# Up-units of the second feed-forward layer multiplied in products of 256 columns

## The chip, the cores and the metric

The kernel runs on one core of one Trainium2 chip. The metric is the device time of one execution in microseconds, from the start of the program to its end. Lower is better.

## What is computed

A two-layer transformer stem (a dilated-attention layer and a latent-attention layer, each followed by a feed-forward network) and then one block of another model, on 512 tokens of width 1024 in float32. The change touches the second of the two feed-forward networks alone:

```
D_MODEL = 1024
SEQ = 512
D_FF = 4 * D_MODEL

def sq_relu_mlp(h, w1, w2):
    a = jax.nn.relu(h @ w1)
    return (a * a) @ w2

        h = rms_norm(x, norm_ffn[i])
        x = x + sq_relu_mlp(h, ffn_w1[i], ffn_w2[i])
```

`h @ w1` is 512 x 1024 by 1024 x 4096; the change is in how half of the tiles of this product are issued for layer `i = 1`.

## The kernel before

**Data.** Everything is kept transposed: a tile has 128 features on the partitions and the 512 tokens along the columns. All weights come as a stream of units of 128 x 1024 (512 KB); each unit is loaded by SyncE into one of four slots of `raw`, rounded to the short format fp32r by ScalarE (`w_hi`, L1069), and what the rounding left is made by VectorE (`w_lo`, L1734). Activations are kept in the same two parts: `h_hi`/`h_lo` for the first feed-forward layer, `g_hi`/`g_lo` for the second.

**A product.** A weight tile of 128 x 128 times a tile of activations is three matmuls of 512 columns into one PSUM bank, in `mm3`: high weights by high activations (L432), high weights by low activations (L433), low weights by high activations (L434). The program has no weight load of its own: each of these calls becomes a weight load (LDWEIGHTS, the engine PEld of the profile) and a matmul (MATMUL, the engine PE). The high weights are loaded for L432 and again for L433. `pairs` reads the columns of the activations in an order that puts column `b` beside column `256 + b`. In other stages the operands are plain float32; a call with such operands shows as two loads and two matmuls.

**A unit.** `unit` waits until the unit's `w_lo` is there and then does the eight tiles of the unit: 24 matmuls of 512 columns, of which the last one tells ScalarE that the bank is ready.

**The feed-forward layer.** `ffn(layer, i)` is one of four chunks: eight up-units (`j` 0 to 7, hidden columns of `h @ w1`) and eight down-units (`j` 8 to 15, of `(a*a) @ w2`). Units 0 and 1 are done together, tile by tile, by `units_together`, as are units 8 and 9; the others go through `unit`. After an up-unit ScalarE takes the bank through the relu (`f_r`, L1199), VectorE squares it (`f_s`, L1921), ScalarE rounds it (`f_hi`, L1204) and VectorE makes the rest (`f_lo`, L1924); units 8 and 9 read these eight tiles in turn. Chunks 1 and 2 of the four are two rounds of a loop, chunks 0 and 3 are written out. Between the up-units 1 and 2 of chunk 0 stand four float32 matmuls that sum squares (L468, L473).

What sets the order is only the order of the program on each engine and the semaphores between them. Nothing is planned or rearranged.

Of the kernel before, what the change touches and what calls it, by code (L numbers as in the profile page):

```python
# [27 lines left out]
KT = D // P  # L28
# [47 lines left out]
def slot(u):  # L76
    if u < R2:
        return u % 3
    return (u - R2) % 4
# [31 lines left out]
def build(nc, stream, x_in, cols_in, crow_in, lam_in, pos_in, ada_in, gate_in, rope_in, consts_in, mask_in, out, stop="all"):  # L111
    with ExitStack() as ctx:
# [6 lines left out]
        def fixed(name, shape, dt=F32):  # L119
            t = at(name, shape, base[0], dt)  # L120
            n = 4
            for s in shape[1:]:
                n *= s
            base[0] += (n + 31) // 32 * 32
            return t
# [11 lines left out]
        w_hi = fixed("w_hi", [P, 4, UNIT], F32R)  # L137
        w_lo = fixed("w_lo", [P, 4, UNIT], F32R)
# [96 lines left out]
        def bank(b, n=512, o=0):  # L235
            return psum[:, b, o:o + n]


        S = {}
# [27 lines left out]
        def after(name, idx):  # L267

            v = idx + 1 + CREDIT.get(name, 0)
            return S[name], (max(v, 0) if isinstance(v, int) else v)  # L270
# [14 lines left out]
        def tile_of(t, sl, w):  # L285
            return t[:, sl, w * P:(w + 1) * P]
# [3 lines left out]
        def pairs(t):  # L290
            return t.rearrange("p (a b) -> p b a", a=2)
# [43 lines left out]
        FFN_IN = ((h_hi, h_lo), (g_hi, g_lo))  # L335
# [90 lines left out]
        def _(pe):  # L426
            credits(pe, "mm", "A_T", "A_PV")

            def mm3(o, whi, wlo, xh, xl, start, stop, read=pairs):

                xh, xl = read(xh), read(xl)
                nc.tensor.matmul(o, whi, xh, start=start, stop=False)  # L432
                nc.tensor.matmul(o, whi, xl, start=False, stop=False)  # L433
                return nc.tensor.matmul(o, wlo, xh, start=False, stop=stop)  # L434

            def unit(u, sl, o, xh, xl, ready=None):

                pe.wait_ge(*after("lo", u))
                for k in range(KT):
                    if ready:  # L440
                        pe.wait_ge(*ready(k))
                    last = mm3(o, tile_of(w_hi, sl, k), tile_of(w_lo, sl, k), xh[:, k, :], xl[:, k, :], k == 0, k == KT - 1)
                last.then_inc(S["mm"], 1)

            def units_together(u, slots, outs, xh, xl, ready, turn=range(KT)):

                pe.wait_ge(*after("lo", u + len(slots) - 1))
                for k in turn:
                    pe.wait_ge(*ready(k))
                    for sl, o in zip(slots, outs):  # L450
                        last = mm3(o, tile_of(w_hi, sl, k), tile_of(w_lo, sl, k), xh[:, k, :], xl[:, k, :], k == turn[0], k == turn[-1])
                        if k == turn[-1]:
                            last.then_inc(S["mm"], 1)
# [7 lines left out]
            def collected_sums(kind, nn):  # L461
                collected_first(kind, nn)
                collected_last(kind, nn)
# [18 lines left out]
            def idle_before(nn):  # L482

                idle(5)
                idle(4, after("N_rst", nn))
                idle(3, after("N_hi", 8 * nn))

            def norm_ready(nn):
                return lambda k: after("N_lo", 8 * nn + k)
# [71 lines left out]
            def a_head(h, par, project=True, attend=True):  # L561
                for j in range(9):
                    n = 9 * h + j
                    if project:
                        pe.wait_ge(*after("A_evac", n - 2))
                        unit(U_A + n, j % 3, bank((par + j) % 2), h_hi, h_lo)
                        if j >= 1:
                            a_post(h, j - 1, par)
                    if attend:
                        if j == 0:  # L570
                            a_post(h - 1, 8, 1 - par)
                        if j in (0, 2):
                            a_scores(h - 1, j, 1 - par)
                        if j in (2, 4):
                            a_transposes(h - 1, j - 2)
                            a_transposes(h - 1, j - 1)
                        if j in (4, 6):
                            a_values(h - 1, j - 4)
                            a_values(h - 1, j - 3)


            def outward(u0, xh, xl, ready, free, kind, nn, b0=0, begun=False, turn=range(KT), first=2):

                if not begun:
                    pe.wait_ge(*free(1))
                    if first > 2:
                        pe.wait_ge(*free(2))
                    units_together(u0, [slot(u0 + i) for i in range(first)], [bank((b0 + i) % 4) for i in range(first)],
                                   xh, xl, ready, turn)
                for o in range(first, KT):  # L590
                    pe.wait_ge(*free(o))
                    unit(u0 + o, slot(u0 + o), bank((o + b0) % 4), xh, xl)
                if kind == "Y":
                    collected_sums(kind, nn)


            def ffn(layer, i, first=False, last=False):
                u0 = (U_F0, U_F1)[layer]
                c = 4 * layer + i
                for j in range(16):  # L600
                    if first and j in (0, 2):
                        pe.wait_ge(*after("R_x", 8 * layer + 5 + j))

                    if j < 4:
                        pe.wait_ge(*after("F_x", 8 * c + j - 4))
                    elif j < 12:
                        pe.wait_ge(*after("F_s", 8 * c + j - 4))
                    else:
                        pe.wait_ge(*after("F_x", 8 * c + j - 12))
                    sl = slot(u0 + j)  # L610
                    if j == 1:
                        units_together(u0 + 16 * i, (slot(u0), sl), (bank(0), bank(1)), *FFN_IN[layer], norm_ready(1 + 2 * layer))
                        if first:
                            collected_sums("N", 1 + 2 * layer)
                    elif 2 <= j < 8:
                        unit(u0 + 16 * i + j, sl, bank(j % 4), *FFN_IN[layer])
                    elif j == 9:
                        units_together(u0 + 16 * i + 8, (slot(u0 + 8), sl), (bank(0), bank(1)), f_hi, f_lo,
                                  lambda k: after("F_lo", 8 * c + k))
                    elif j >= 10:  # L620
                        unit(u0 + 16 * i + j, sl, bank(j % 4), f_hi, f_lo)
                if last and layer == 1:
                    collected_sums("N", 4)
                    idle_before(4)
# [118 lines left out]
            a_out(1, 7)  # L743
            outward(U_AO, a_oh, a_ol, None, lambda o: after("R_x", o - 4), "N", 1, begun=True)
            ffn(0, 0, first=True)
            with pe.Fori(1, FFN_CHUNKS - 1) as i:
                ffn(0, i)
            ffn(0, FFN_CHUNKS - 1, last=True)


# [252 lines left out]
            for n in range(2, 20):  # L1003
                u = U_MI + n
                pe.wait_ge(*after("M_ev", n - 2))
                pe.wait_ge(*after("lo", u))
                for k in range(KT):
# [9 lines left out]
                    if at_step in SOFT_AT:  # L1017
# [5 lines left out]
                        if m >= 2:  # L1023
                            c_values(m - 2)
                    last = mm3(bank(n % 2), tile_of(w_hi, slot(u), k), tile_of(w_lo, slot(u), k), h_hi[:, k, :], h_lo[:, k, :],
                               k == 0, k == KT - 1)
# [1580 lines left out]
```

## Time and profile before

| what | value |
|---|---|
| time, median of 3 runs | 2382.67 us (2382.32 to 2382.8) |
| span of the profiled execution, first to last instruction | 2380.2 us |
| TensorE matmul (PE) busy | 2336.3 us, 98% of the span |
| weight loads (PEld) busy | 1981.6 us, 83% |
| VectorE busy | 1440.3 us, 61% |
| ScalarE busy | 1038.3 us, 44% |
| matmuls and weight loads | 11342 of each |

The profiled execution's own time is given as its span; the time of a run also holds what lies outside the first and last instruction, 2.5 us between this span and the median. A matmul's bar in the trace is longer than its share of the time, because the next one begins while it still drains: the step from one start to the next is what counts, not the bar. The times of weight loads overlap with those of matmuls.

### The profile page before, as it was taken

The page shows a single profiled execution, that of the slowest core. Times are in us where ns is not written, and L with a number is a line of the kernel's source. Part 1 is how long each engine was busy: PE and PEld are TensorE (multiplying, and loading weights), DVE is VectorE, ACT ScalarE, POOL GpSimd, SP SyncE. Part 2 cuts the span into 40 slices and gives each one's busy share as a digit, 9 for nine tenths or more (in the row PEclk, how much of TensorE's full clock was granted, in tenths as well). Part 3 has the DMA queues.
Part 4 walks back from the last instruction along what each step waited for, and adds up shares of the span by engine and source line. Part 5 has one row for each costly group of instructions (what it writes and reads, how often), then busy time and mean ns, then how long its engine had stood idle before and what let it go on. Part 6 is the DMA issues. An engine that isn't in the chain of part 4 may idle for free.

```text
span 2380.2 us, 30886 instructions
## 1 busy us (share of the span) xinstructions
PE 2336.3 (98%) x11342; PEld 1981.6 (83%) x11342; DVE 1440.3 (61%) x2073; ACT 1038.3 (44%) x1562; POOL 0.2 (0%) x4
## 2 busy tenths in 40 slices
PE   7999999999999999999999999999999999999999
PEld 5788888888888886888888888888877677888887
DVE  7877777767566677867566575333356986433333
ACT  5655555544233347854223333323346565322333
POOL 0000000000000000000000000000000000000000
PEclk9999999999999999999999999999999999999999
DMA  4222222235444531024444533332322112323231
GB/s 156 80 80 80 79 79 77 77 103 177 140 161 159 174 117 64 1 72 168 159 150 159 177 102 108 105 100 95 115 71 67 58 54 71 97 94 110 93 111 54
DMA packets 71246, 249.57 MB, mean 105 GB/s; under 512 B 9824, under 2 KB 10336, under 8 KB 70752
## 3 DMA queue, kind: packets, MB, share of 16 engines
q1 hardware_dynamic: 68912, 247.28, 31.1%
q8 instruction: 74, 1.21, 0.2%
q10 hardware_dynamic: 2224, 0.79, 0.1%
q14 instruction: 36, 0.29, 0.0%
HBM read 245.94 MB, written 2.10 MB: 104 GB/s over the span
## 4 chain that ended last, share of the span: by engine, by line
PE 91%; DVE 5%; ACT 3%; issue 1%; DMA 0%; SPq 0%; ACTq 0%; DVEq 0%
PE psum L432 27%; PE psum L434 27%; PE psum L433 27%; PE psum L496 2%; PE psum L885 1%; PE psum L527 1%; PE psum L556 1%; PE psum L549 1%; PE psum L939 1%; DVE w_lo L1734 1%; PE psum L989 1%; DVE x L2249 0%; PE psum L969 0%; PE psum L532 0%; DVE y L2247 0%
## 5 line engine op out<-in xcount | busy, mean ns | idle before, releaser
L432 PE MATMUL psum<-h_hi,w_hi 128*128 128x512 f32 x1768 | 681.6, 386 | 7.6 <-DVE w_lo L1734 2.7
L433 PE MATMUL psum<-h_lo,w_hi 128*128 128x512 f32 x1768 | 670.1, 379 | 0.0
L434 PE MATMUL psum<-h_hi,w_lo 128*128 128x512 f32 x1768 | 670.1, 379 | 0.0
L1069 ACT ACTIVATE w_hi<-raw 128x1024 fp32r<-128x1024 f32 x385 | 403.2, 1052 | 454.8 <-PE psum L434 445.0
L1734 DVE TENSOR_TENSOR w_lo<-raw,w_hi 128x1024 fp32r<-128x1024 f32 x385 | 466.0, 1220 | 133.3 <-ACT w_hi L1069 131.9
L432 PEld LDWEIGHTS psum<-h_hi,w_hi 128*128 128x128 f32 x1768 | 334.2, 189 | 62.5 <-issue 9.3
L433 PEld LDWEIGHTS psum<-h_lo,w_hi 128*128 128x128 f32 x1768 | 334.3, 189 | 47.6 <-issue 2.6
L434 PEld LDWEIGHTS psum<-h_hi,w_lo 128*128 128x128 f32 x1768 | 334.2, 189 | 47.4
L2227 DVE TENSOR_TENSOR s_s<-s_g,psum 128x512 f32<-128x512 f32 x44 | 30.3, 688 | 275.6 <-issue 224.2
L432 PE MATMUL psum<-f_hi,w_hi 128*128 128x512 f32 x512 | 194.0, 379 | 0.0
L433 PE MATMUL psum<-f_lo,w_hi 128*128 128x512 f32 x512 | 194.0, 379 | 0.0
L434 PE MATMUL psum<-f_hi,w_lo 128*128 128x512 f32 x512 | 194.0, 379 | 0.0
L432 PE MATMUL psum<-s_hi,w_hi 128*128 128x512 f32 x352 | 133.4, 379 | 0.0
L433 PE MATMUL psum<-s_lo,w_hi 128*128 128x512 f32 x352 | 133.4, 379 | 0.0
L434 PE MATMUL psum<-s_hi,w_lo 128*128 128x512 f32 x352 | 133.4, 379 | 0.0
L1199 ACT ACTIVATE f_r<-psum 128x512 f32<-128x512 f32 x64 | 38.1, 595 | 207.6 <-PE psum L434 207.5
L1948 DVE TENSOR_TENSOR nrm<-psum,rst 128x512 f32<-128x512 f32 x64 | 44.2, 691 | 128.2 <-PE psum L434 128.0
L434 PEld LDWEIGHTS psum<-f_hi,w_lo 128*128 128x128 f32 x512 | 96.8, 189 | 13.8
L432 PEld LDWEIGHTS psum<-f_hi,w_hi 128*128 128x128 f32 x512 | 96.8, 189 | 13.7
L433 PEld LDWEIGHTS psum<-f_lo,w_hi 128*128 128x128 f32 x512 | 96.8, 189 | 13.7
L1921 DVE TENSOR_TENSOR f_s<-f_r,psum 128x512 f32<-128x512 f32 x64 | 43.9, 686 | 101.5 <-ACT f_r L1199 101.4
L1224 ACT ACTIVATE s_g<-psum 128x512 f32<-128x512 f32 x44 | 26.2, 596 | 175.6 <-PE psum L434 175.6
(343 smaller groups left out, 3252.8 us busy)
## 6 DMA issues: line engine op xcount, KB each, us to landing
raw<-stream SPq DMA_DIRECT2D x385, 512.0 KB, 3.5
ada_raw<-ada_in SPq DMA_DIRECT2D x72, 512.0 KB, 4.0
x<-x_in SPq DMA_DIRECT2D x2, 1024.0 KB, 6.4
out<-x SPq DMA_DIRECT2D x8, 256.0 KB, 2.4
a_mask<-mask_in SPq DMA_DIRECT2D x1, 1024.0 KB, 9.4
crow<-crow_in SPq DMA_DIRECT2D x2, 512.0 KB, 4.5
gatew<-gate_in ACTq DMA_DIRECT2D x2, 256.0 KB, 3.7
a_cos<-rope_in SPq DMA_DIRECT2D x1, 256.0 KB, 7.8
```

The source lines that it names most:

```text
L432: nc.tensor.matmul(o, whi, xh, start=start, stop=False)
L433: nc.tensor.matmul(o, whi, xl, start=False, stop=False)
L434: return nc.tensor.matmul(o, wlo, xh, start=False, stop=stop)
L496: last = nc.tensor.transpose(o[:, b * P:(b + 1) * P], src[:, b * P:(b + 1) * P], ident[:])
L527: nc.tensor.matmul(psum[32 * t:32 * t + 32, 2 + r % 2, 0:256], q[:, 0, r * P + 32 * t:r * P + 32 * t + 32], a_k0[:, par, t * P:t * P + 256 ...
L1069: A(w_hi[:, slot(u0), :], raw[:, slot(u0), :], ACT.Copy).then_inc(S["hi"], 1)
L1199: A(stored(f_r[:, j % 2, :]), by_parity(bank(j % 4)), ACT.Relu).then_inc(S["F_r"], 1)
L1224: A(stored(s_g[:, q % 2, :]), by_parity(bank(j % 6)), ACT.Silu).then_inc(S["Sw_g"], 1)
L1734: V.tensor_tensor(w_lo[:, sl, :], raw[:, sl, :], f32(w_hi[:, sl, :]), ALU.subtract).then_inc(S["lo"], 1)
L1921: V.tensor_tensor(stored(f_s[:, j % 2, :]), stored(f_r[:, j % 2, :]), by_parity(bank(j % 4)), ALU.mult).then_inc(S["F_s"], 1)
L1948: V.tensor_tensor(nrm[:, 1, :], down, rst[:, 1, :], ALU.mult).then_inc(S["F_t"], 1)
L2227: V.tensor_tensor(stored(s_s[:, q % 2, :]), stored(s_g[:, q % 2, :]), by_parity(bank((2 * jj + 1) % 6)), ALU.mult).then_inc(S["Sw_s"], 1)
```

## The change

For the second layer alone (`layer == 1`) the up-units with `j` from 2 to 7 go through a new function, `unit_halves`. It issues the same three products for each weight tile, but each of them as two matmuls of 256 columns, the first half of the bank and then the second half, one behind the other with the same weights. Units 0 and 1, the down-units and the first layer are as before. No wait, no semaphore and no buffer changes.

```diff
+            def mm3_halves(o, whi, wlo, xh, xl, start, stop):
+
+                xh, xl = pairs(xh), pairs(xl)
+                for w, x_, first, last in ((whi, xh, start, False), (whi, xl, False, False), (wlo, xh, False, stop)):
+                    for c in range(2):
+                        b = slice(c * 128, (c + 1) * 128)
+                        ins = nc.tensor.matmul(o[:, c * 256:(c + 1) * 256], w, x_[:, b, :], start=first and c == 0, stop=last and c == 1,
+                                               skip_group_check=True)
+                return ins
+
+            def unit_halves(u, sl, o, xh, xl):
+
+                pe.wait_ge(*after("lo", u))
+                for k in range(KT):
+                    last = mm3_halves(o, tile_of(w_hi, sl, k), tile_of(w_lo, sl, k), xh[:, k, :], xl[:, k, :], k == 0, k == KT - 1)
+                last.then_inc(S["mm"], 1)
+
...
                     elif 2 <= j < 8:
-                        unit(u0 + 16 * i + j, sl, bank(j % 4), *FFN_IN[layer])
+                        (unit, unit_halves)[layer](u0 + 16 * i + j, sl, bank(j % 4), *FFN_IN[layer])
```

The order on TensorE where chunk 0 of the second layer passes from the sums of squares to up-unit 2, before (a row is a line of the program, what is written and read, and the shape; weight loads are not listed):

```order
L468 MATMUL psum<-nrm,ones 128x512
L473 MATMUL psum<-sq,ones 128x512
L432 MATMUL psum<-g_hi,w_hi 128x512
L433 MATMUL psum<-g_lo,w_hi 128x512
L434 MATMUL psum<-g_hi,w_lo 128x512
```

The same place of the changed program, in which the sums have the lines L485 and L490 and x2 is two matmuls in a row:

```order
L485 MATMUL psum<-nrm,ones 128x512
L490 MATMUL psum<-sq,ones 128x512
L442 MATMUL psum<-g_hi,w_hi 128x256 x2
L442 MATMUL psum<-g_lo,w_hi 128x256 x2
L442 MATMUL psum<-g_hi,w_lo 128x256 x2
```

Each matmul of 512 columns has become two of 256 in its own place; nothing else stands between them.

The order on TensorE where up-unit 7 of a chunk ends and down-units 8 and 9 begin, before:

```order
L432 MATMUL psum<-g_hi,w_hi 128x512
L433 MATMUL psum<-g_lo,w_hi 128x512
L434 MATMUL psum<-g_hi,w_lo 128x512
L432 MATMUL psum<-f_hi,w_hi 128x512
L433 MATMUL psum<-f_lo,w_hi 128x512
```

And in the changed program:

```order
L442 MATMUL psum<-g_hi,w_hi 128x256 x2
L442 MATMUL psum<-g_lo,w_hi 128x256 x2
L442 MATMUL psum<-g_hi,w_lo 128x256 x2
L432 MATMUL psum<-f_hi,w_hi 128x512
L433 MATMUL psum<-f_lo,w_hi 128x512
```

The down-units follow as before, in matmuls of 512 columns. Per chunk 6 units of 24 products are affected, in four chunks 576 products: 1152 matmuls and 1152 weight loads stand in the place of 576 of each. The instructions of the other engines are the same.

## Rows read from the trace of the kernel before

**Rows 1.** The page: busy time per engine, and the granted clock in 40 slices.

```profile
PE 2336.3 (98%) x11342; PEld 1981.6 (83%) x11342; DVE 1440.3 (61%) x2073; ACT 1038.3 (44%) x1562; POOL 0.2 (0%) x4
...
PEclk9999999999999999999999999999999999999999
```

**Rows 2.** The page: the chain that ended last, by engine.

```profile
PE 91%; DVE 5%; ACT 3%; issue 1%; DMA 0%; SPq 0%; ACTq 0%; DVEq 0%
```

**Rows 3.** Windows: busy us and count per engine, clock; layer two, then two dense stretches.

```profile
1078.00:1413.00 335.00, 334.82 (x1546) 291.74 (x1544) 211.93 (x279) 106.12 (x140) 0.00 (x0) 1.00 0.46 156
497.50:503.87 6.37, 6.37 (x65) 4.76 (x65) 3.72 (x12) 1.79 (x5) 0.00 (x0) 1.00 0.03 9
496.54:508.91 12.37, 12.15 (x101) 9.67 (x100) 6.38 (x22) 5.80 (x13) 0.00 (x0) 1.00 0.09 34
```

**Rows 4.** Tile g_hi: duration min/median/max in ns, first and last start in us.

```profile
L432 PEld LDWEIGHTS psum<-g_hi,w_hi x256: 189/189/190, 1078.4 to 1369.5; 128*128 128x128 f32 x128
L432 PE MATMUL psum<-g_hi,w_hi x256: 379/379/780, 1078.6 to 1369.7; 128*128 128x512 f32 x128
```

**Rows 5.** Timeline of weight loads in an up-unit: start us, duration us.

```profile
1109.85 0.19 PEld L432 LDWEIGHTS psum<-g_hi,w_hi 128*128 128x128 f32 x1
1110.07 0.19 PEld L433 LDWEIGHTS psum<-g_lo,w_hi 128*128 128x128 f32 x1
```

**Rows 6.** Timeline of matmuls at the same place.

```profile
1109.63 0.38 PE L433 MATMUL psum<-g_lo,w_hi 128*128 128x512 f32 x1
1109.85 0.38 PE L434 MATMUL psum<-g_hi,w_lo 128*128 128x512 f32 x1
...
1112.87 0.38 PE L433 MATMUL psum<-g_lo,w_hi 128*128 128x512 f32 x1
```

**Rows 7.** The chain in order of time: start us, us, what; short and long float32 matmuls.

```profile
98.38 0.87 PE psum L496 x8
...
364.48 1.79 PE psum L556 x16
...
958.58 0.89 PE psum L885 x8
...
1089.09 0.86 PE psum L468 x2
1089.95 0.86 PE psum L473 x2
...
1800.15 3.43 PE psum L939 x8
```

**Rows 8.** Timeline of weight loads from plain float32 (L885) to fp32r (L862, L863).

```profile
958.31 0.97 PEld L885 LDWEIGHTS psum<-b_pt,b_v 128*128 128x128 f32 x8
959.20 0.19 PEld L862 LDWEIGHTS psum<-b_kh,h_hi 128*128 128x128 f32 x1
959.31 0.19 PEld L863 LDWEIGHTS psum<-b_kl,h_hi 128*128 128x128 f32 x1
959.53 0.19 PEld L864 LDWEIGHTS psum<-b_kh,h_lo 128*128 128x128 f32 x1
```

**Rows 9.** Timeline of weight loads after a wait of TensorE.

```profile
34.50 0.19 PEld L432 LDWEIGHTS psum<-h_hi,w_hi 128*128 128x128 f32 x1 [0.27 <-DVE h_lo L1765]
34.61 0.19 PEld L433 LDWEIGHTS psum<-h_lo,w_hi 128*128 128x128 f32 x1
```

**Rows 10.** Timeline of ScalarE and VectorE behind up-unit 7 of chunk 0.

```profile
1121.92 0.60 ACT L1199 ACTIVATE f_r<-psum 128x512 f32<-128x512 f32 x1 [3.12 <-PE psum L434]
...
1126.04 0.68 DVE L1924 TENSOR_TENSOR f_lo<-f_s,f_hi 128x512 fp32r<-128x512 f32 x1
```

**Rows 11.** Waits from 1078 to 1413 us: total us, times, longest; then SyncE's own.

```profile
ACT f_r L1199 <- PE psum L434: 104.0, 27, 12.9
ACT w_hi L1069 <- PE psum L434: 86.5, 18, 9.2
DVE nrm L1948 <- PE psum L434: 67.0, 27, 3.8
...
SPq L368 <- DVE w_lo L1734: 185.5, 63, 7.5
```

**Rows 12.** DMA queues from 1078 to 1161 us: packets, MB, share of 16 engines.

```profile
q8 instruction: 3, 0.05, 0.3%
```

## The prediction

> **What bounds the kernel now.** I read the page first. TensorE is busy for 98% of the span, the chain that ended last lies on it for 91%, and its granted clock stands at the full level, 2.4 GHz, in every slice [rows 1, 2]. The windows view of the stage that changes says it more sharply: from 1078 to 1413 us TensorE is busy for 334.82 of 335.00 us [rows 3]. The waits there are all of others for TensorE: ScalarE's relu waits 104.0 us for matmuls, VectorE 67.0 us, and SyncE holds its loads back for free slots for 185.5 us [rows 11]. So whatever the changed matmuls gain or lose is gained or lost in full, and only the step from one matmul to the next matters.
>
> That step is read from starts, not from bars. Fifteen steps of 512 columns take 1112.87 - 1109.63 = 3.24 us, 216 ns each [rows 6]. A long baseline gives it closer. From the first to the last L432 on `g_hi`, 1078.6 to 1369.7 us [rows 4], lie three chunks of 384 products and 64 tiles less one of three more, 1341 products, and the two pairs of sums of 0.86 us each [rows 7]: (291.1 - 1.72) / 1341 = **215.8 ns**. A load starts when the matmul before its own starts (both rows at 1109.85 us) [rows 5, 6], so a load has 215.8 ns to be ready in, and is never what is waited for.
>
> **The change part by part.** It takes away 576 matmuls of 512 columns with their loads, and puts 1152 of 256 columns with 1152 loads in their place. Nothing else moves. Call h the step of a half; the change costs 576 x (2h - 215.8 ns). The trace has no full-array matmul of 256 columns, so h is put together from what a step must contain, and is the longer of two things.
>
> *The stream of columns.* For plain float32 the trace has the same engine at two widths: eight transposes of 128 columns in 0.87 us, 108.8 ns each, and eight passes of 512 columns in 3.43 us, 428.8 ns each [rows 7]. That is 0.833 ns for a column and some 2 ns per matmul. The fp32r matmul takes half as long per column: 215.8 ns are 512 x 0.4167 = 213.3 ns and 2.5 ns. So 256 columns stream in 106.7 + 2.5 = 109.2 ns. A half can't go below 106.7 ns even if the 2.5 ns vanished; that would be 576 x (213.3 - 215.8) = -1.4 us, 0.06%, so a gain that can be told from nothing is excluded by the column rate.
>
> *The load of the weights.* Each half loads its 128 x 128 tile again, as L433 does now right behind L432 with the same `w_hi` tile [rows 5]. How long must a load be awaited? After an idle TensorE, L432's load starts at 34.50 us and the next one, which marks the start of L432's stream, at 34.61 [rows 9]: 110 ns. In the bursts of short float32 matmuls, whose own stream would allow 109 ns, the step is longer: 0.89 us for eight (L885) and 1.79 us for sixteen (L556) [rows 7]. Rounding allows 110.6 to 111.9 ns by the first row and 111.6 to 112.2 ns by the second; both hold between 111.6 and 111.9, and I take 111.7 ns. The transposes with the same columns and a step of 108.8 ns show that the stream isn't what makes 111.7; the load is. An fp32r load costs the same: L862's load starts at 959.20 us and its stream at 959.31 [rows 8].
>
> A half of 256 columns is therefore in the same position as a float32 pass of 128: stream 109.2 ns, load 111.7 ns, and the load decides by a little. h = 111.7 ns: 2 x 111.7 - 215.8 = 7.6 ns per product, x 576 = **4.4 us**. With the last half of a unit the next load is of a 512-column matmul and costs the same 111.7 ns, so nothing is to be added at the seams.
>
> The Trainium skill, "TensorE: Matmul & The Clock Gate", section "Back-to-back issue gap", gives N / 2.4 + 2.5 ns at full clock, from which the stream alone would follow: 109.2 ns for a half, and 1.5 us for the change. The trace agrees with it at 512 columns (215.8 ns) and disagrees at L885, whose step is 111.7 ns for reasons outside that formula. The same section names sustained steps for pairs of load and matmul, 81 ns at 128 columns and 131 ns at 512, which would speak against halving; the 215.8 ns of this trace contradict the second of them.
>
> *What comes at no cost.* The last up-unit ends at 1121.92 us, and its `f_lo` is done at 1126.04 + 0.68 = 1126.72 us [rows 10]. Units 8 and 9 need it only for their eighth tile, after 42 products, 42 x 0.2158 = 9.1 us, at 1131.0 us: 4.3 us of cover, which the change leaves alone, as the down-units keep their pace. If it were gone, each microsecond missing would cost one per chunk, 4 in all. Up-units become slower by 24 x 7.6 ns = 0.18 us each, so ScalarE, VectorE and the loads have that much more time and none is later for TensorE. Instruction fetches: three packets in a chunk take 0.3% of 16 engines' 83 us, some 4 us, 1.3 us each [rows 12]. With the instructions twice as dense one is needed about every 14 us in place of 28 us, and 1.3 us still fit ten times.
>
> **Sum.** The profiled span is 2380.2 us and the median 2382.67, 2.5 us outside the instructions that the change doesn't touch. 2380.2 + 4.4 + 2.5 = **2387.1 us**, 0.18% over now. What a measurement of this kernel can tell from no change is about 0.2%, 4.8 us. The forecast stands just inside it.
>
> **The rivals.**
>
> *The stream decides.* If a half is paced by its columns, or if the second load of the same tile overlaps more than those of L885, h is 109.2 ns and the cost 576 x 2.6 ns = 1.5 us: 2384.2 us. For it: the loads after an idle engine took 110 ns or a little less [rows 9], nearer to 109. Against it: every dense burst of loads that are not transposes reads 111.7 ns. Chance 0.11.
>
> *The instructions aren't supplied fast enough* (the slower side). A unit now asks for a load and a matmul each 111.7 ns for 5.4 us on end; now it is 215.8 ns. What the trace shows beyond short bursts: 65 matmuls and 65 loads in 6.37 us, 98 ns a pair, and 101 in 12.37 us, 122 ns a pair [rows 3]. The first speaks against this rival, but some of its instructions may have been waiting ready from the slower stretch ahead, and six units on end take 32 us. If the 122 ns of the longer stretch were the supply's, the change would cost 576 x (244.9 - 215.8) = 16.8 us: 2399.5 us. It decides, and passes 0.2%, from a supply step of 112.1 ns. The Trainium skill, in "What happens when you issue a matmul" of "TensorE: Matmul & The Clock Gate", names some 62 ns per matmul where its sequencer decodes in software; for a load and a matmul that would be 124 ns, about the same 2401 us, and the 98 ns of the first stretch are against it. Chance 0.12.
>
> *The load is slower behind a stream at full rate.* All bursts that show 111.7 ns have float32 streams, which take a column in 0.833 ns. Behind an fp32r stream, at twice that rate, a load is only known to be done within 215.8 ns. Were both to share what they read with, h would lie between 111.7 and 215.8 ns; at the upper end the cost is 576 x 215.8 = 124 us: 2507 us. Against it: the loads' bars are 189 ns behind fp32r streams, and no longer behind float32 ones (8 bars with 7 steps of 111.7 fill the 0.97 us of L885 with 0.19 for one) [rows 5, 8]. It too passes 0.2% from h = 112.1 ns. Chance 0.10.
>
> *Something downstream gets earlier or later* by more than I see, either way: 0.05, of it 0.02 for faster.
>
> **How the numbers follow.** The forecast, load-paced, has 0.62, with its own range of 2386.0 to 2388.2 us (h from 111.3 to 112.3 ns with the readings' rounding). The stream's 2384.2 and the milder half of the supply's and the load's cases, up to about 10 us over now, bring it to 8 in 10: 2384.0 to 2393.0 us. Slower by over 0.2%: both slower rivals 0.22, a fifth of the forecast's own 0.62 that ends above 2387.4, 0.12, and 0.02 from downstream, 0.36. Faster by over 0.2%: 0.02. The rest, 0.62, is within 0.2%.
>
> **What would show it.** In the profile after, L442 has 1152 matmuls and as many loads; in the timeline of loads inside an up-unit 2 to 7 of layer two, steps of 111 or 112 ns with no idle of PEld between them. Steps of 109 ns would be the stream; steps that are even at 109 to 112 for the first microseconds of a unit and then longer, with PE idle on issue, the supply; even steps well above 112, the slowed load. The stage from unit 2 to the last chunk's unit 7 grows by 4.4 us and nothing outside it. The forecast is wrong if h is off: each nanosecond of h is 1.15 us.

## The result and the profile after

The changed kernel takes 2386.41 us (median of 18 runs, 2385.55 to 2386.99), the kernel before 2382.22 us in the same comparison (18 runs, 2381.27 to 2382.8). The ratio is 1.0018, with a 95% interval of 1.0011 to 1.0025: 4.2 us slower, between 2.6 and 6.0. The forecast was 4.4 us.

The page of the changed kernel answers to [rows 1, 2]:

```profile
span 2385.0 us, 32038 instructions
...
PE 2341.1 (98%) x11918; PEld 2001.7 (84%) x11918; DVE 1440.1 (60%) x2073; ACT 1040.1 (44%) x1562; POOL 0.2 (0%) x4
...
PEclk9999999999999999999999999999999999999999
...
PE 91%; DVE 5%; ACT 3%; issue 1%; DMA 0%; SPq 0%; ACTq 0%; DVEq 0%
```

There are 576 more matmuls and 576 more loads (11918 against 11342), and TensorE is busy 4.8 us longer; VectorE's and ScalarE's busy times are within 2 us of what they were, and the clock is as it was. The windows view of the stage, as in [rows 3]:

```profile
1078.00:1417.40 339.40, 339.40 (x2124) 311.98 (x2122) 211.63 (x278) 106.47 (x140) 0.00 (x0) 1.00 0.47 155
```

TensorE still never stops in it. How long the stage is, is read from the tiles. The last matmul of the stage on `f_hi` in the kernel before:

```profile
L432 PE MATMUL psum<-f_hi,w_hi x512: 379/379/379, 592.4 to 1411.2; 128*128 128x512 f32 x171
```

Tile `f_hi` of the changed kernel, with duration min/median/max in ns and first and last start in us:

```profile
L432 PE MATMUL psum<-f_hi,w_hi x512: 379/379/382, 592.8 to 1416.0; 128*128 128x512 f32 x171
```

Tile `g_hi` of the same kernel:

```profile
L442 PEld LDWEIGHTS psum<-g_hi,w_hi x384: 189/192/192, 1090.7 to 1374.5; 128*128 128x128 f32 x192
L442 PE MATMUL psum<-g_hi,w_hi x384: 272/275/673, 1090.8 to 1374.6; 128*128 128x256 f32 x192
...
L432 PE MATMUL psum<-g_hi,w_hi x64: 379/379/379, 1079.1 to 1342.4; 128*128 128x512 f32 x64
```

From the first L432 on `g_hi` to the last on `f_hi` it was 1411.2 - 1078.6 = 332.6 us [rows 4] and is 1416.0 - 1079.1 = 336.9 us: 4.3 us more. The rest of the span's 4.8 us is half a microsecond ahead of the stage, which begins at 1079.1 us in place of 1078.6. Kernels that are the same up to there differ by more: below, the first half of a product starts at 1090.0 us in the run with uneven pieces and at 1091.0 in the one with thirds.

The timeline of weight loads in a middle up-unit, where [rows 5] had one load every 216 ns:

```profile
1109.36 0.30 PEld L442 LDWEIGHTS psum<-g_lo,w_hi 128*128 128x128 f32 x2
1109.59 0.30 PEld L442 LDWEIGHTS psum<-g_hi,w_lo 128*128 128x128 f32 x2
...
1111.37 0.30 PEld L442 LDWEIGHTS psum<-g_lo,w_hi 128*128 128x128 f32 x2
```

From 1109.36 to 1111.37 us lie 18 loads: 2.01 / 18 = 0.1117, **111.7 ns a step**, with no idle of PEld in between. The x2 are the two halves, and a row's 0.30 is one step of 0.11 and one bar of 0.19.

The waits of the stage:

```profile
ACT w_hi L1086 <- PE psum L434: 86.7, 18, 9.2
ACT f_r L1216 <- PE psum L442: 73.0, 23, 3.3
DVE nrm L1965 <- PE psum L434: 66.9, 27, 3.8
DVE f_s L1938 <- ACT f_r L1216: 56.6, 23, 7.9
ACT f_r L1216 <- PE psum L434: 35.0, 4, 12.9
```

The longest are for TensorE, as in [rows 11]; the fourth is VectorE's for ScalarE's relu. No wait of TensorE is among them. ScalarE's relu waits 73.0 + 35.0 = 108.0 us in place of 104.0, about what TensorE has become slower.

### The profile page after: what moved, and what is told of

It reads as the page before. It is cut to its first block, busy times and chain, and to the rows that moved or that the text cites. A ratio compares the mean times of both kernels' runs of the same rounds, so it can differ in the third digit from the quotient of the medians.

```text
span 2385.0 us, 32038 instructions
## 1 busy us (share of the span) xinstructions
PE 2341.1 (98%) x11918; PEld 2001.7 (84%) x11918; DVE 1440.1 (60%) x2073; ACT 1040.1 (44%) x1562; POOL 0.2 (0%) x4
## 4 chain that ended last, share of the span: by engine, by line
PE 91%; DVE 5%; ACT 3%; issue 1%; DMA 0%; SPq 0%; ACTq 0%; DVEq 0%
PE psum L432 25%; PE psum L433 25%; PE psum L434 25%; PE psum L442 5%; PE psum L513 2%; PE psum L902 1%; PE psum L544 1%; PE psum L573 1%; PE psum L566 1%; PE psum L956 1%; DVE w_lo L1751 1%; PE psum L1006 1%; DVE x L2266 0%; PE psum L986 0%; PE psum L549 0%
## 5 line engine op out<-in xcount | busy, mean ns | idle before, releaser
L432 PE MATMUL psum<-h_hi,w_hi 128*128 128x512 f32 x1768 | 682.3, 386 | 7.5 <-DVE w_lo L1751 2.7
L1086 ACT ACTIVATE w_hi<-raw 128x1024 fp32r<-128x1024 f32 x385 | 404.2, 1054 | 454.4 <-PE psum L434 445.1
L432 PEld LDWEIGHTS psum<-h_hi,w_hi 128*128 128x128 f32 x1768 | 334.6, 189 | 62.6 <-issue 9.3
L432 PE MATMUL psum<-f_hi,w_hi 128*128 128x512 f32 x512 | 194.1, 379 | 0.0
L432 PE MATMUL psum<-s_hi,w_hi 128*128 128x512 f32 x352 | 133.4, 379 | 0.0
L432 PEld LDWEIGHTS psum<-f_hi,w_hi 128*128 128x128 f32 x512 | 96.8, 189 | 13.6
L433 PEld LDWEIGHTS psum<-f_lo,w_hi 128*128 128x128 f32 x512 | 96.8, 189 | 13.6
```

Of the source, the lines that this page charges most:

```text
L1086: A(w_hi[:, slot(u0), :], raw[:, slot(u0), :], ACT.Copy).then_inc(S["hi"], 1)
```

## The experiments

The measured interval, 2.6 to 6.0 us, leaves out the 1.5 us of a half paced by its stream, but not a cost that each half has for another reason: the forecast rests on a difference of 2.5 ns, 109.2 ns for the stream and 111.7 ns for the load. Three theories were told apart. **Load-paced**: a step is the longer of the weight load (111.7 ns for 128 columns of weights) and the stream (0.4167 ns a column and 2.5 ns). **Fixed cost**: every matmul of a cut product costs 5.0 ns on top of its columns, whatever the load (a whole product shows 2.5 ns). **Supply**: a load and a matmul can't be had faster than every 111.7 ns. Each kernel below is the changed kernel with another edit; all but `all_halves` change the same 24 units alone.

Uneven pieces, thirds, quarters and the quarters with 64 and with 96 columns of weights were executed once each, and the kernel before scatters from 2381.0 to 2382.7 us. So the length of the stage, read in every profile from the first L432 on `g_hi` to the last on `f_hi`, stands beside the times:

| kernel | stage, us | more than before | by load-paced |
|---|---|---|---|
| before | 332.6 | | |
| the change | 336.9 | 4.3 | 4.3 |
| uneven pieces | 366.2 | 33.6 | 33.6 |
| thirds | 401.2 | 68.6 | 68.7 |
| quarters | 470.3 | 137.7 | 133.1 |
| quarters, loop written out | 465.6 | 133.0 | 133.1 |
| halves, 64 columns of weights | 334.0 | 1.4 | 1.5 |
| whole products, 64 columns | 332.6 | 0.0 | 0.0 |
| quarters, 64 columns | 347.7 | 15.1 | 10.0 |
| quarters, 96 columns, written out | 404.2 | 71.6 | 71.5 |
| half by half | 337.0 | 4.4 | 4.3 |

The last column takes 58.3 and 85.0 ns, the steps found below, for loads of 64 and 96 columns. Two rows stand out, by 4.6 and 5.1 us; both are taken up under "The loop".

**Uneven pieces.** The pieces have 384 and 128 columns; as many matmuls, loads and columns as in the change.

```diff
-                    for c in range(2):
-                        b = slice(c * 128, (c + 1) * 128)
-                        ins = nc.tensor.matmul(o[:, c * 256:(c + 1) * 256], w, x_[:, b, :], start=first and c == 0, stop=last and c == 1,
+                    for c, (p, q) in enumerate(zip([0, 192, 256], [0, 192, 256][1:])):
+                        ins = nc.tensor.matmul(o[:, 2 * p:2 * q], w, x_[:, p:q, :], start=first and c == 0, stop=last and c == 1,
...
```

> The pieces of a product are 384 and 128 columns instead of two of 256; the same count of matmuls and loads. Load-paced (step = the longer of a weight load, 111.7 ns, and columns x 0.4167 + 2.5 ns): 162.5 + 111.7 = 274.2 ns a product, 576 x (274.2 - 215.8) = 33.6 us, about 2415.8 us. Fixed cost per matmul (columns x 0.4167 + 5.0 ns, no limit by the load): 223.3 ns as with even halves, 2386.5 us. Supply of instructions at 111.7 ns a pair: as load-paced.

Measured: 2415.23 us against 2381.68 before, 33.6 us more. The weight loads of a middle up-unit:

```profile
1109.47 0.30 PEld L441 LDWEIGHTS psum<-g_lo,w_hi 128*128 128x128 f32 x2
...
1110.84 0.30 PEld L441 LDWEIGHTS psum<-g_hi,w_hi 128*128 128x128 f32 x2
```

Five products in 1.37 us, 274 ns each, which is the sum that load-paced gives: 162.5 ns for the long piece and 111.7 for the short one. The fixed cost falls. By this theory what is lost is the room behind the short piece: its columns need 56 ns, and the next load isn't there before 111.7. The rows shown give the sum alone, not how the two pieces share it.

**Thirds and quarters.** The same edit with the cuts `[0, 86, 171, 256]` and `[0, 64, 128, 192, 256]`.

> Three matmuls of 172, 170 and 170 columns in the place of each of 512. Load-paced: 3 x 111.7 = 335.1 ns, 576 x 119.3 = 68.7 us, 2450.9 us. Fixed cost: 228.3 ns, 7.2 us, 2389.4 us. If fp32r streams of less than 256 columns took the 0.833 ns per column of plain float32: 145.8 + 2 x 144.1 = 434 ns, 125.7 us, 2507.9 us.

> Four matmuls of 128 columns in the place of each of 512. Load-paced: 4 x 111.7 = 446.8 ns, 576 x 231.0 = 133.1 us, 2515.3 us. Fixed cost: 213.3 + 4 x 5.0 = 233.3 ns, 10.1 us, 2392.3 us. Supply: as load-paced.

Measured: thirds 2451.26 us, 69.4 us over the 2381.87 before; quarters 2520.09 us, 138.4 us over 2381.68. Weight loads of thirds:

```profile
1109.41 0.41 PEld L441 LDWEIGHTS psum<-g_hi,w_hi 128*128 128x128 f32 x3
...
1110.75 0.41 PEld L441 LDWEIGHTS psum<-g_lo,w_hi 128*128 128x128 f32 x3
```

And of quarters:

```profile
1109.37 0.53 PEld L441 LDWEIGHTS psum<-g_hi,w_lo 128*128 128x128 f32 x4
...
1110.71 0.41 PEld L441 LDWEIGHTS psum<-g_hi,w_lo 128*128 128x128 f32 x3
```

In both it is 12 steps in 1.34 us, 111.7 ns, for pieces of 170 or 172, of 128 and, in the change, of 256 columns. Down to 128 columns an fp32r stream doesn't become slow enough to matter. Quarters took 5.3 us more than 576 x (4 x 111.7 - 215.8) = 133.1 us; that is taken up below.

**Fewer columns of weights.** Load-paced and supply agree on all of this. A load of 64 columns parts them. In `halves_64_weights` the pieces are even halves, in `quarters_64_weights` quarters, in `whole_64_weights` whole products. These kernels leave out half of the output rows of the 24 units. The edit, against the form with cuts:

```diff
-                        ins = nc.tensor.matmul(o[:, 2 * p:2 * q], w, x_[:, p:q, :], start=first and c == 0, stop=last and c == 1,
+                        ins = nc.tensor.matmul(o[0:64, 2 * p:2 * q], w[:, 0:64], x_[:, p:q, :], start=first and c == 0, stop=last and c == 1,
```

> Even halves, but the weights of each are only columns 0 to 63 of the tile, so the output rows 64 to 127 of these units are left out; matmuls stream the same 256 columns. Load-paced: a load of half the columns takes some 58 ns and no longer decides, the step falls to the stream's 109.2 ns, a product to 218.4 ns, cost 1.5 us, 2383.7 us. Fixed cost or supply: the step stays at 111.7 ns, 2386.5 us.

> A control for the run with 64 columns of weights: whole products of 512 columns with weights of 64 columns (output rows 64 to 127 of these units left out). All theories: 215.8 ns a product, the time of before, 2382.2 us.

> Quarters of 128 columns with weights of 64 columns (output rows 64 to 127 of these units left out). Load-paced: load some 58 ns, stream 128 x 0.4167 + 2.5 = 55.8 ns, step 58 ns, product 233 ns, 10 us, 2392 us. Supply at 111.7 ns a pair: 133 us, 2515 us. Narrow fp32r streams at 0.833 ns per column: step 109.2 ns, 127 us, 2509 us.

Measured: halves 2383.27 us (ratio 1.0007, 0.9998 to 1.0016), whole 2382.03 us (1.0001, 0.9992 to 1.001), both against 2381.68; quarters 2396.92 us, 15.0 us over 2381.87. The intervals of the first two overlap, so it is their traces that decide: the stage of whole products is as long as before, 332.6 us, so fewer columns of weights alone change nothing, and that of halves is 334.0 us. Weight loads of halves with 64 columns of weights:

```profile
1109.44 0.24 PEld L441 LDWEIGHTS psum<-g_lo,w_hi 128*64 128x64 f32 x2
...
1110.75 0.24 PEld L441 LDWEIGHTS psum<-g_lo,w_hi 128*64 128x64 f32 x2
```

And of quarters with 64 columns of weights:

```profile
1109.58 0.31 PEld L441 LDWEIGHTS psum<-g_lo,w_hi 128*64 128x64 f32 x4
...
1110.98 0.14 PEld L441 LDWEIGHTS psum<-g_lo,w_hi 128*64 128x64 f32 x1
```

The halves' step is 1.31 / 12 = 109.2 ns: with the load out of the way it is the stream's, and 576 x (2 x 109.2 - 215.8) = 1.5 us is what the stage has grown by. The quarters' is 1.40 / 24 = 58.3 ns, just above the 55.8 ns of 128 columns. So a load and a matmul can be had every 58 ns, and the supply isn't what makes 111.7. The time is 15.0 us over, where 576 x (4 x 58.3 - 215.8) = 10.0 us was expected; the rest is the loop's, as in quarters.

**A third point for the load.** Quarters with weights of 96 columns, and the loop written out (see below).

> As quarters_written_out, with weights of 96 columns (output rows 96 to 127 of these units left out). If the load takes its columns / 1.2 + 5 ns, as 111.66 ns at 128 and 58.33 ns at 64 say, the step is 85.0 ns, a product 340 ns, 576 x 124.2 = 71.5 us, about 2453 us.

Measured: 2453.75 us, 72.1 us over 2381.7. Its weight loads:

```profile
1109.55 0.42 PEld L441 LDWEIGHTS psum<-g_lo,w_hi 128*96 128x96 f32 x4
...
1110.91 0.25 PEld L441 LDWEIGHTS psum<-g_hi,w_lo 128*96 128x96 f32 x2
```

1.36 / 16 = 85.0 ns. With 58.3, 85.0 and 111.7 ns for 64, 96 and 128 columns of weights the load is on a line: 0.833 ns a column and 5.0 ns.

This line holds for the loads of ordinary matmuls. The transposes have loads of 128 columns too, and a step of 108.8 ns that is shorter than 111.7. Their loads differ: in the kernel before, the mean bar of a load (the second number between the strokes, in ns) is 141 for a transpose and 192 for a dense burst of float32 matmuls.

```profile
L556 PEld LDWEIGHTS psum<-a_pt,a_v 128*128 128x128 f32 x128 | 14.9, 192 | 0.0
L496 PEld LDWEIGHTS psum<-ident,a_s 128*128 128x128 f32 x128 | 14.7, 141 | 1.3 <-DVE a_s L1841 0.5
```

Why a transpose's load is shorter was not tried.

**The order of the halves.** First the three matmuls of the first half, then those of the second.

```diff
-                for w, x_, first, last in ((whi, xh, start, False), (whi, xl, False, False), (wlo, xh, False, stop)):
-                    for c in range(2):
-                        b = slice(c * 128, (c + 1) * 128)
+                for c in range(2):
+                    b = slice(c * 128, (c + 1) * 128)
+                    for w, x_, first, last in ((whi, xh, start, False), (whi, xl, False, False), (wlo, xh, False, stop)):
...
```

> The three matmuls of the first half of the columns, then the three of the second half: the same tile is loaded twice in a row less often (2 of 6 loads repeat the load before, in place of 4 of 6). Load-paced with every load done in full: the same as the change, 2386.4 us. If a repeated load were cheaper or dearer than a new one, the time moves by 576 x the difference / 3 or so.

Measured: 2386.1 us against 2381.87, ratio 1.0018 (1.0008 to 1.0027), as the change, and the stage is as long to a tenth or so of a microsecond. This order makes 384 of the 1152 halves load a new tile where the change repeats one (the expectation's third of 576 is too low). A half can't go below its stream's 109.2 ns, so a cheaper repeat could have shown as 384 x 2.5 ns = 1.0 us at most, at the edge of what the times tell. Quarters show it better: three of their four loads repeat the one before behind a stream of 56 ns, and each takes 111.7 ns. A load that repeats the one before is as dear as a new one.

**Everything in halves.** `mm3` hands all its paired products to `mm3_halves`, in all stages.

```diff
             def mm3(o, whi, wlo, xh, xl, start, stop, read=pairs):
 
+                if read is pairs:
+                    return mm3_halves(o, whi, wlo, xh, xl, start, stop)
```

> All products of mm3 that read in pairs are done in halves, in both layers and everywhere else: 9120 matmuls of 512 columns become 18240. Load-paced: 9120 x 7.5 ns = 68 us, 2450.6 us, a little less where TensorE now waits for others. Supply that falls behind in long dense stretches: clearly more than that, with PE idle on issue.

Measured: 2458.55 us against 2381.87, ratio 1.0321 (1.0301 to 1.0342), 76.7 us more. The profile has 20534 - 11342 = 9192 more matmuls, so 9192 products were halved, where the expectation had 9120; load-paced gives 68.9 us, and 7.8 us are left. The waits of TensorE name a place:

```profile
PE psum L444 <- issue: 7.4, 4, 2.8
```

Four times, 7.4 us in all, it had nothing to do and waited for nothing that the profile shows; before, there was no such row for its matmuls. One of them in the timeline:

```profile
329.32 0.60 PE L515 MATMUL psum<-ident,a_raw 128*128 128x128 f32 x4
332.74 0.79 PE L444 MATMUL psum<-h_hi,w_hi 128*128 128x256 f32 x2 [2.82 <-issue]
```

**The loop.** Quarters have one such stop of 2.6 us, where chunk 2, the second round of the loop over chunks 1 and 2, has just begun. So have quarters with 64 columns of weights, at 1255.74 us, of 2.71 us. The timeline of quarters:

```profile
1314.49 0.38 PE L432 MATMUL psum<-g_hi,w_hi 128*128 128x512 f32 x1
1317.51 0.48 PE L433 MATMUL psum<-g_lo,w_hi 128*128 128x512 f32 x1 [2.63 <-issue]
...
1318.44 0.63 PE L433 MATMUL psum<-g_lo,w_hi 128*128 128x512 f32 x1
1318.87 0.63 PE L434 MATMUL psum<-g_hi,w_lo 128*128 128x512 f32 x1
...
1321.67 0.38 PE L432 MATMUL psum<-g_hi,w_hi 128*128 128x512 f32 x1
```

And the windows of quarters there:

```profile
1314.70:1317.30 2.60, 0.17 (x1) 0.00 (x0) 1.19 (x2) 0.00 (x0) 0.00 (x0) 1.00 0.30 72
1317.30:1321.00 3.70, 3.49 (x9) 2.79 (x10) 0.00 (x0) 0.00 (x0) 0.00 (x0) 0.60 0.37 132
```

After the stop the granted clock falls to 1.2 GHz (0.60 in the mean of the second window), and a step of 512 columns is 1318.87 - 1318.44 = 0.43 us, twice as long. The stop puts 3.02 us in the place of one step of 0.22, and the 11 steps behind it take 4.16 us in place of 2.37: 2.8 and 1.8 us, 4.6 of the 4.7 by which the stage is longer than with the loop written out.

The DMA view names what else is particular to that round. Its queue q8 carries instructions, in packets of 16 KB. In the second round of quarters, 1312 to 1420 us:

```profile
q8 instruction: 8, 0.13, 0.5%
```

And within the stop alone, 1314.7 to 1317.4 us:

```profile
q8 instruction: 1, 0.02, 2.2%
```

In the second round of the kernel before (1244 to 1327 us), of the change (1245 to 1328), of thirds (1282 to 1390) and of the feed-forward loop of `all_halves` (1280.7 to 1378) the view has no packet of q8 at all. So the instructions of those rounds are not loaded a second time, and those of quarters are. That TensorE's stop is the wait for the first of these packets fits both views, but no row names it as what ended the wait.

One kernel more takes the loop away from the second layer and leaves all else of quarters:

```diff
             ffn(1, 0, first=True)
-            with pe.Fori(1, FFN_CHUNKS - 1) as i:
+            for i in range(1, FFN_CHUNKS - 1):
                 ffn(1, i)
```

> As quarters, with the four chunks of the second layer written out on TensorE in place of the loop over chunks 1 and 2. Steps stay at 111.7 ns. If the 5 us that quarters took beyond 4 x 111.66 ns a product are the fetch of instructions at the start of the loop's second round (2.6 us of idle, then matmuls at 1.2 GHz), they are gone: about 2515 us. If they come from dense instructions as such, 2520 us as before.

Measured: 2514.82 us against 2381.7, 133.1 us more, to the tenth what 4 x 111.7 ns give, and no wait on issue in its profile. The surplus was the loop's. Written out, the instructions come in packets all along (13 from 1195 to 1430 us) without a stop, so loading as such doesn't stop TensorE; it does where it falls on the start of a round. The round of quarters has 96 + 1152 + 384 = 1632 loads and matmuls; the rounds of thirds (1344), of the feed-forward chunks in `all_halves` (1536), and of the change (1056) show no such stop. The four stops of `all_halves` are in the loop over the heads: two at the start of its second round (202.32 and 205.67 us) and two at that of its third (332.74 and 335.81 us). Its round grew from about 1350 loads and matmuls, for which the kernel before loads no packet of q8 in the last two rounds, to about 2210. These two rounds take 260.2 us (199.06 to 459.25) in place of 240.1 (196.82 to 436.94), of which their 864 halved products are 6.5; the stops and the lower clock behind them (0.50 from 202.9 to 209.7 us) make the other 13.6. The rest of the kernel grew by some 6 us less than load-paced gives; the expectation had foreseen less where TensorE waits for others, but how much of it that is was not traced.

## Why the prediction was right

**The bound.** TensorE alone sets the time of the stage: right; 339.40 us busy of 339.40, and 576 products at 7.5 ns more come out in the end in full. The sentence that the waits there are all for TensorE was too wide: the same view of the kernel before also has VectorE waiting 52.4 us for ScalarE's relu and ScalarE 24.7 us for VectorE. None of them is a wait of TensorE, so the sum doesn't depend on it.

**The step of a half.** 111.7 ns, taken from bursts of float32 matmuls [rows 7]: right to the tenth, 2.01 us for 18 loads. That it is the load which makes it, and not the stream or a cost per matmul, was argued from the transposes' 108.8 ns. The argument holds only because the loads of transposes are shorter, which the prediction didn't say: a load of 111.7 ns would have paced them too. It is now shown: with 64 columns of weights the step falls to 109.2 ns, the value given for the stream. The float32 passes of 128 columns were the right stand-in, since they have the same load and a stream as long.

**The sum.** 576 x 7.6 ns = 4.4 us; the stage grew by 4.3 us, the medians lie 4.2 us apart. The absolute 2387.1 us is 0.7 above the measured 2386.41; 0.45 us of that is that the kernel before came out at 2382.22 in this comparison and not 2382.67. The forecast's own range was given too wide: h from 111.3 to 112.3 ns makes 3.9 to 5.1 us, 2386.6 to 2387.8 us.

**What was said to cost nothing** did. The relu behind up-unit 7 of chunk 0 starts at 1123.52 us and its `f_lo` is done at 1128.33, 4.8 us later, as it was before [rows 10]; down-unit 8 begins at 1123.32 us and needs it after 9.1 us, so 4.1 us of cover are left. The prediction's 4.3 us were counted from the relu's start, 0.2 us behind that of the down-unit. It also spread the loading of instructions evenly over the chunks. That cost the forecast nothing, but it isn't so: the second round of the loop loads none here, and loads them anew, with a stop, once the round is long enough.

**The rivals.** *The stream decides*: fell, by the steps. *The supply*: fell for the instructions in a row, since 58.3 ns a pair hold through whole units, against the 122 and 124 ns by which it was priced. It exists in a form that the prediction didn't have: at the start of a loop's later rounds, when the round is long enough; the change's isn't. The 122 ns of [rows 3] were the mix of that stretch, not a limit. *The slower load behind a full-rate stream*: fell; the load keeps 111.7 ns behind fp32r streams of 128 to 256 columns. The prediction drew on the bars of 189 ns against it; the bars behind halves are 192 ns and say nothing of the step, so the argument was weaker than its outcome.

The rule of the Trainium skill that was weighed ("TensorE: Matmul & The Clock Gate", "Back-to-back issue gap") holds for the stream: 256 / 2.4 + 2.5 = 109.2 ns is what halves with 64 columns of weights take. The formula leaves the load out, and with it two thirds of the price. The same page's section "LDWEIGHTS (loading the stationary operand)" has the columns divided by 1.2 in ns, which is the slope found here; the 5.0 ns on top are this trace's.

## What to carry to other kernels

Where each matmul brings its own load, its step is the longer of two times, the stream of its columns and the load of its weights; here they cross at (111.7 - 2.5) / 0.4167, some 262 columns of fp32r, so a matmul may be cut down to about that at next to no cost and below it each piece costs a whole load. Price such a cut from a place in the trace where the load already decides, even if it is of another type and stage, and test the price by an edit that shortens the load alone. Don't take it from transposes. When instructions are multiplied inside a loop, look at the start of the second round as well: for idle on issue, and in the DMA view for packets of instructions where there were none.

## What was not expected of the hardware

A loop whose round had 1632 loads and matmuls stopped TensorE for 2.6 us at its second round and loaded its instructions again, and one with 1536 did neither; the stop then cost another 1.8 us in matmuls at 1.2 GHz. Written out, the same work took 5.3 us less, 4.7 of them in this stage. Where between 1536 and 1632 it begins, and whether the count of the loop alone decides, was not tried. Nor was it tried what the 5.0 ns that a load takes beyond its columns are, or why the load of a transpose is shorter.
